# A mixture-of-experts layer: the 64 expert lists packed into 42 passes instead of 52, rows without a token skipped, and the last pass added from the matmul unit

## Chip, cores, metric

One core of one Trainium2 chip. The metric is the device time of one launch in microseconds (us), the median of several runs.

## What is computed

One decoder step for 512 prompt tokens, 16 meta tokens and 8 sample tokens of 1024 features: a state-space part and a retention part (not touched by the change), an output projection, and then a mixture of experts (MoE). Its core in the reference:

```python
scores = jax.nn.sigmoid((h @ w_router).astype(jnp.float32))
...
_, eidx = lax.top_k(jnp.where(emask, sel, -jnp.inf), TOP_K)      # 8 of 64 experts
...
hg = jnp.einsum('td,edf->tef', h, w_gate_e)                      # 1024 -> 256
hu = jnp.einsum('td,edf->tef', h, w_up_e)
act = jax.nn.silu(hg) * hu * gates[..., None]
routed = jnp.einsum('tef,efd->td', act, w_down_e)                # 256 -> 1024
shared = (jax.nn.silu(h @ w_gate_sh) * (h @ w_up_sh)) @ w_down_sh
```

The layer's output is x + routed + shared, and the final output is its rmsnorm. 520 tokens (the prompt and the samples) go through the experts, 8 experts each, so the lists of the 64 experts hold 4160 rows together. On the reference's own inputs the router gives, sorted by length, lists of 243, 175, 146, 130, 116, 105, 105, 105, 95, 89, ... rows; the 26th (counted from 0) has 64, the 59th 28 and the last 7. Everything is float32. The three matrices of one expert are 3 x 1024 KB, 201 MB for all 64.

## The kernel before

The first 400 us compute the two mixers, the output projection, the router and, on the chip, the ranking of the experts by the length of their lists. A **rank** below is the place of an expert in this order. The expert of a rank is read from a table (`order_i`) into a register, so the program is fixed and the experts are not.

The MoE stage works in **passes** (`UNITS`, `make_units`, L83). A pass has 128 row places. A list of rank 0 to 3 gets 256 places (two passes), one of rank 4 to 31 gets 128 places (a pass), and lists of rank 32 to 63 get 64 places each, two to a pass. That makes 52 passes (`NU`): 36 that hold one list and 16 that hold two. A *visit* (`VISITS`) is an expert in the order in which its weights are needed. What a list has beyond its places would be done afterwards in `overflow`, in a loop that is skipped when nothing is left.

What a pass u does, by engine:

- SyncE (SP) loads the weights (`sync_weights`, L358) into one of 6 slots of 3 MB. Visit v waits for the slot of visit v-6: gate and up for the last up matmul that used it (`pe_gu`), down for the last down matmul (`pe_down`).
- ScalarE (ACT) loads the pass's piece of the lists four passes ahead (`act_list`, L347), one DMA for each list of the pass, and copies one half of PSUM results.
- VectorE (DVE) makes from it the row indices and gates (`dve_meta`). A place without a token gets an index of 2048 (`DUMP`) or more. DVE also copies the other halves, and actT (L654).
- GpSimd (POOL) gathers the 128 rows of the tokens from `h2_rows` in HBM, three passes ahead (`pool_gather`, L440; `bounds_check` is 1543 there, so an index of 2048 and above is out of bounds), and scatters the 128 result rows into `sum_rows` in HBM with an addition (`pool_scatter`, L449; `bounds_check` is 2175 there, so the rows from 2048 on are written). Scatter u waits until scatter u-1 has landed.
- TensorE (PE) runs, in this order: the gate and up matmuls of u (`pe_up`), the transposes of the rows of u+1 (`pe_rows`), the down matmuls of u-1 (`pe_down`), the transposes of the activations of u (`pe_act`). All the matmuls are recorded at L912, row transposes at L929, activation transposes at L950. A matmul of float32 leaves two records in the trace.

A pair's two lists are in separate columns of the array (0 to 63 and 64 to 127) and in separate rows of a PSUM bank. Rows of its upper half go to a second copy of the sum, 1024 rows further (`ACC2`), because a token could stand in both lists, and two additions to one row in one DMA would lose one of them.

After the last pass POOL waits for the last scatter, asks for overflow, and sets `all_added`; then SP loads both copies of the sums (10 DMAs, L401), DVE adds them (L734), ACT squares them and takes the root (L534), DVE scales (L907), SP stores. The table of lists is filled with zeros in the first 60 us, as are the gaps between row 520 and row 1024 of `h2_rows` and `sum_rows`, through three more DMAs (L1202).

## Time and profile before

| | us |
|---|---|
| median of 3 runs (1156.03 to 1158.11) | 1157.16 |
| the profiled execution, its own time | 1158.64 |
| its span, from the first to the last instruction | 1156.8 |
| PE busy | 1013.1 (88%) |
| DVE, POOL, ACT busy | 435.0, 261.6, 200.5 |
| mean granted TensorE clock | 0.941 of full speed |

The profiled execution's time is 1.84 us more than its span. "Busy" is the union of an engine's instructions, and for DMA the mean over the core's 16 DMA engines. Of one more view: the DMA share of a stretch near or a little over 1 means that all 16 engines always had packets in work.

### The profile page before, as it was taken

How to read it: one execution, taken by the hardware profiler on the slowest of the kernel's cores; microseconds unless marked ns; L12 is line 12 of the kernel's file. 1: busy time of each engine (PE TensorE's matmuls, PEld its weight loads, DVE VectorE, ACT ScalarE, POOL GpSimd, SP SyncE). 2: the span in 40 equal slices, each digit the busy share in tenths (PEclk: the TensorE clock that was granted, in tenths of full speed). 3: DMA queues.
4: the chain of work that ended last, by engine and by line, in shares of the span. 5: the costliest groups of instructions: out<-in, count | busy, mean ns of one | idle time of the engine just before them, and what ended most of it. 6: DMA issues, size and time to landing. Idle time of an engine off the chain costs nothing.

```text
span 1156.8 us, 11769 instructions
## 1 busy us (share of the span) xinstructions
PE 1013.1 (88%) x3825; PEld 504.2 (44%) x3825; DVE 435.0 (38%) x1036; ACT 200.5 (17%) x401; POOL 261.6 (23%) x320
## 2 busy tenths in 40 slices
PE   5989987979888977899999979988999969997950
PEld 3564555556445533344444434433444424443420
DVE  6866467766936541223121212212122112221214
ACT  5150032312222211111111101111111101111112
POOL 2900056030300661021212112112021202222110
PEclk9989998989988988899999989999899979998995
DMA  9932020221353259699999999999999999999846
GB/s 330 407 148 74 1 73 1 91 67 74 109 206 126 74 227 415 258 356 367 380 368 380 367 386 383 366 381 380 373 375 349 377 379 353 340 371 369 293 87 225
DMA packets 72175, 308.98 MB, mean 267 GB/s; under 512 B 18529, under 2 KB 19585, under 8 KB 47153
## 3 DMA queue, kind: packets, MB, share of 16 engines
q1 hardware_dynamic: 48112, 261.07, 56.7%
q0 software_dynamic: 16256, 45.40, 16.2%
q10 hardware_dynamic: 7744, 1.73, 0.8%
q8 instruction: 32, 0.52, 0.2%
q14 instruction: 31, 0.25, 0.1%
HBM read 262.60 MB, written 55.79 MB: 275 GB/s over the span
## 4 chain that ended last, share of the span: by engine, by line
PE 68%; DMA 12%; DVE 8%; issue 6%; ACT 4%; POOL 2%; SPq 1%; POOLq 0%; DVEq 0%; ACTq 0%
PE bank L912 43%; PE bank L1839 20%; DMA sum_rows<-arena,xs 6%; PE bank L929 4%; DVE arena L1487 3%; DMA sum_rows<-arena 2%; POOL expert_lists L459 2%; DMA arena<-h_rows,xs 1%; PE bank L950 1%; DMA arena<-sum_rows 1%; ACT arena L1156 1%; ACT arena L1143 1%; DVE arena L1818 1%; DVE arena L1800 1%; DMA qkv_samples<-arena 1%
## 5 line engine op out<-in xcount | busy, mean ns | idle before, releaser
L912 PE MATMUL bank<-arena 128*128 128x512 f32 (+4 forms) x1890 | 630.2, 586 | 54.6 <-issue 34.2
L912 PEld LDWEIGHTS bank<-arena 128*128 128x128 f32 (+2 forms) x1890 | 249.2, 169 | 358.7 <-issue 343.6
L1839 PE MATMUL bank<-arena 128*128 128x512 f32 (+9 forms) x1208 | 308.3, 442 | 30.6 <-DVE arena L1487 8.3
L1839 PEld LDWEIGHTS bank<-arena 128*128 128x128 f32 (+4 forms) x1208 | 172.4, 191 | 160.0 <-issue 128.4
L449 POOL DMA_INDIRECT sum_rows<-arena,xs x52 | 81.7, 1571 | 497.8 <-DVE xs L667 301.0
L638 DVE SCALAR_TENSOR_TENSOR arena<-arena,xs,bank 128x256 f32<-128x256 f32 x52 | 34.7, 667 | 365.1 <-issue 326.6
L635 DVE COPY arena<-bank 128x512 f32<-128x512 f32 x52 | 36.0, 692 | 141.8 <-PE bank L912 130.8
L513 ACT ACTIVATE arena<-bank 128x256 f32<-128x256 f32 x52 | 20.0, 385 | 392.4 <-PE bank L912 287.3
L1487 DVE TENSOR_TENSOR arena<-arena 64x512 f32<-64x512 f32 (+8 forms) x79 | 69.6, 882 | 6.5 <-DMA arena<-o_samples 3.9
L440 POOL DMA_INDIRECT arena<-h_rows,xs x52 | 54.2, 1042 | 60.0 <-DVE xs L667 45.2
L929 PEld LDWEIGHTS bank<-ident,arena 128*128 128x128 f32 x416 | 47.3, 140 | 31.8 <-issue 28.0
L459 POOL DMA_INDIRECT expert_lists<-arena,ncim x40 | 40.0, 1000 | 91.5 <-issue 88.3
L507 ACT COPY arena<-bank 128x512 f32<-128x512 f32 x52 | 30.5, 586 | 152.4 <-PE bank L912 114.3
L929 PE MATMUL bank<-ident,arena 128*128 128x128 f32 x416 | 54.9, 275 | 0.2 <-DMA arena<-h_rows,xs 0.2
L626 DVE COPY arena<-bank 128x512 f32<-128x512 f32 x52 | 35.5, 682 | 13.6 <-DMA sum_rows<-arena 13.5
L499 ACT COPY arena<-bank 128x512 f32<-128x512 f32 x52 | 30.5, 586 | 34.6 <-PE bank L929 28.5
L950 PEld LDWEIGHTS bank<-ident,arena 128*128 128x128 f32 x104 | 13.3, 140 | 31.7 <-issue 31.2
L1295 POOL COPY prm<-prm 128x8 f32<-128x8 f32 x2 | 0.4, 188 | 118.1 <-PE bank L1839 97.2
L1487 DVE TENSOR_TENSOR arena<-bank,cosin 128x512 f32<-128x512 f32 (+1 forms) x24 | 14.4, 602 | 26.8 <-PE bank L1839 14.5
L654 DVE COPY arena<-bank 128x256 f32<-128x256 f32 x52 | 21.6, 415 | 0.0
L950 PE MATMUL bank<-ident,arena 128*128 128x128 f32 x104 | 20.7, 281 | 0.3 <-DVE arena L638 0.3
L1850 PE MATMUL bank<-ident,arena 128*128 128x128 f32 (+1 forms) x40 | 7.8, 383 | 13.3 <-DVE arena L1514 10.0
(230 smaller groups left out, 513.4 us busy)
## 6 DMA issues: line engine op xcount, KB each, us to landing
arena<-in_w_gate_e SPq DMA_DIRECT2D x64, 1024.0 KB, 20.4
arena<-in_w_up_e SPq DMA_DIRECT2D x64, 1024.0 KB, 33.6
arena<-in_w_down_e SPq DMA_DIRECT2D x64, 1024.0 KB, 30.8
arena<-in_w_in SPq DMA_DIRECT2D x5, 2048.0 KB, 12.4
expert_lists<-arena SPq DMA_DIRECT2D x1, 8482.5 KB, 28.8
sum_rows<-arena SPq DMA_DIRECT2D x9, 512.0 KB, 26.2
arena<-in_x_prompt SPq DMA_DIRECT2D x8, 512.0 KB, 5.7
arena<-in_w_out SPq DMA_DIRECT2D x2, 2048.0 KB, 8.2
```

Of the source, the lines that this page charges most:

```text
L440: pool.indirect_dma_start(xg[u % XBUF], None, h2_dram, bass.IndirectOffsetOnAxis(idx[:, u % IDX:u % IDX + 1].bitcast(U32), axis=0), bounds ...
L449: pool.indirect_dma_start(sum_dram, bass.IndirectOffsetOnAxis(idx[:, u % IDX:u % IDX + 1].bitcast(U32), axis=0), ys[u % 2], None, bounds_c ...
L459: pool.indirect_dma_start(tab, bass.IndirectOffsetOnAxis(dest[0:r_, n_, k:k + 1].bitcast(U32), axis=0), grow[0:r_, i, :], None, bounds_che ...
L499: nc.scalar.copy(xgT[u % 2][:, 0:4, :], bank[0][:, :].rearrange("p (k t) -> p k t", k=4)).then_inc(s("a_xgt"), 1)
L626: nc.vector.tensor_copy(xgT[u % 2][:, 4:8, :], bank[1][:, :].rearrange("p (k t) -> p k t", k=4)).then_inc(s("d_xgt"), 1)
L635: nc.vector.tensor_copy(ys[u % 2][:, 512:1024], bank[5][:, :]).then_inc(s("d_ys"), 1)
L638: return nc.vector.scalar_tensor_tensor(actg[b].rearrange("t (k p) -> t p k", k=2), sil[b].rearrange("t (p k) -> t p k", k=2), gate_col, g ...
L912: return nc.tensor.matmul(o, l, r, start=start, stop=stop, skip_group_check=True)
L929: t = nc.tensor.transpose(bank[k // 4][:, P * (k % 4):P * (k % 4) + P], xg[u % XBUF][:, P * k:P * k + P], ident[:])
L950: t = nc.tensor.transpose(bank[3][:, P * k:P * k + P], actg[u % 2][:, P * k:P * k + P], ident[:])
L1487: return v.tensor_tensor(o, a_, b_, op)
L1839: return nc.tensor.matmul(o, l, r, start=start, stop=stop, skip_group_check=True, **kw)
```

## The change

1. **Packing.** `CAPACITY` gives 256, 192, 160, 160 places to ranks 0 to 3, 128 to ranks 4 to 7, 96 to ranks 8 to 25, 64 to ranks 26 to 59 and 32 to ranks 60 to 63. Each pass is cut into blocks of one width (128, 64 or 32 columns): 9 passes of one whole block, 14 of two blocks of 64 (13 pairs of light lists, and the last 64 places of rank 1 beside a light list), 18 of four blocks of 32 (`thirds`: 96 places of one list in three blocks, and in the fourth 32 places of another, which in 12 of them is one half of a 64-place list spread over two passes), and the last pass with a light list alone in one block of 64. Together 42 passes.
2. **No spare rows.** A place without a token gets an index of 8192 (`FAR`) or more for gather and for scatter, and both DMAs now have `oob_is_err=False` and bounds that exclude it (519 and 1039). The second copy of `h2_rows` and the spare rows of `sum_rows` are gone, with their stores and the three DMAs of zeros; the two copies of the sum are 520 rows apart, and `ACCS` says which of them each list of a pass goes to.
3. **Tables.** The expert and the validity of each place of each pass come from 8 small matmuls more in `sort()` with a table of ranks that SP loads (`c_sel`), and fewer DVE operations in `sort_tables`. `dve_meta` has one small operation more.
4. **actT** is copied by ACT (`act_turn`), not DVE, between ACT's half of the down results and its list loads.
5. **The end.** The last pass (a light list alone) is not scattered. SP waits for the scatter of the last but one (`scattered` of 41) and loads both copies of the sums; POOL adds the two copies (L507 of the changed kernel); PE multiplies the result rows of the last pass with a one-hot matrix (`onehot`, 1 where the row of the pass belongs to the token), 8 matmuls of 128 x 512 and 4 of 8 x 256; DVE adds that from PSUM and goes on as before, tile by tile.

```diff
@@ make_units
-    for g in range(HEAVY // 2):
-        for r in heavy[2 * g:2 * g + 2]:
-            for first in range(0, rank_capacity(r), 128):
-                units.append(((r, 0, 128, first),))
-        units.append(((HEAVY + 2 * g, 0, 64, 0), (HEAVY + 2 * g + 1, 64, 64, 0)))
+CAPACITY = [256, 192, 160, 160] + 4 * [128] + 18 * [96] + 34 * [64] + 4 * [32]
+    thirds = lambda r: [(r, 32 * n, 32, 32 * n) for n in range(3)]
+    split = [[thirds(mids.pop(0)) + [(r, 96, 32, 32 * h)] for h in range(2)] for r in [light.pop(0) for _ in range(6)]]
+    both = [[thirds(mids.pop(0)) + [(r, 96, 32, 0)]] for r in least]
+    pairs = [[[(r, 64 * h, 64, 0) for h, r in enumerate(light[n:n + 2])]] for n in range(0, len(light), 2)]
@@ moe_sync
+            sp.wait_ge(s("pe_down"), NT + NU - 1)
+            sp.dma_start(gain_f, ins["final_norm"].partition_broadcast(P)).then_inc(s("ld_gain"), 16)
+            sp.wait_ge(s("scattered"), 16 * (NU - 1))
+            for n_, i in enumerate(LATE):
+                load_sums(sp, n_, f"ld_tok{i}")
             overflow(sp, sync_more)
-            sp.wait_ge(s("pe_down"), NT + NU)
-            sp.dma_start(gain_f, ins["final_norm"].partition_broadcast(P)).then_inc(s("ld_gain"), 16)
-            sp.wait_ge(s("all_added"), 1)
@@ pool_scatter
-            pool.indirect_dma_start(sum_dram, bass.IndirectOffsetOnAxis(idx[:, u % IDX:u % IDX + 1].bitcast(U32), axis=0),
-                                    ys[u % 2], None, bounds_check=DUMP + P - 1, compute_op=ALU.add
+            pool.indirect_dma_start(sum_dram, bass.IndirectOffsetOnAxis(idx_a[:, u % IDX:u % IDX + 1].bitcast(U32), axis=0),
+                                    ys[u % 2], None, bounds_check=NACC * TT - 1, oob_is_err=False, compute_op=ALU.add
                                     ).then_inc(s("scattered"), 16)
@@ moe_pool
-            for u in range(NU):
+            for u in range(NU - 1):
                 if u + XBUF < NU:
                     pool_gather(pool, u + XBUF)
                 pool_scatter(pool, u)
-            pool.wait_ge(s("scattered"), 16 * NU)
             overflow(pool, pool_more)
-            pool.memset(marks[:, 4:5], 0.0).then_inc(s("all_added"), 1)
+            for n_, i in enumerate(LATE):
+                r_ = rows_of(n_)
+                pool.wait_ge(s(f"ld_tok{i}"), 80 if i == TE else 64)
+                pool.tensor_tensor(fin[0][0:r_, n_, :], fin[0][0:r_, n_, :], fin[1][0:r_, n_, :], ALU.add
+                                   ).then_inc(s("pre_added"), 1)
@@ act_unit
+            act_turn(act, u)
             if u + LISTS < NU:
                 act_list(act, u + LISTS)
@@ moe_pe, after the last pass
+            for n_, i in enumerate(LATE):
+                if n_ == NT - 1:
+                    pe.wait_ge(s("d_sum"), 1)
+                rows = ys[(NU - 1) % 2]
...
+                    for hf in range(2):
+                        t = mmul(bank[LAST_BANK[n_] + hf][:, :], onehot[:, P * i:P * i + P], rows[:, 512 * hf:512 * hf + 512],
+                                 True, True)
+                t.then_inc(s("pe_last"), 1)
```

PE's order in the MoE stage, three passes of the kernel before (a list alone, a pair, a list alone). L912 is up (x8, or x16 for a pair) and down (x4, or x8), L929 the row transposes of the next pass, L950 the activation transposes:

```order
L912 MATMUL bank<-arena 128x512 x8
L929 MATMUL bank<-ident,arena 128x128 x8
L912 MATMUL bank<-arena 128x512 x4
L950 MATMUL bank<-ident,arena 128x128 x2
L912 MATMUL bank<-arena 64x512 x16
L929 MATMUL bank<-ident,arena 128x128 x8
L912 MATMUL bank<-arena 128x512 x4
L950 MATMUL bank<-ident,arena 128x128 x2
L912 MATMUL bank<-arena 128x512 x8
L929 MATMUL bank<-ident,arena 128x128 x8
L912 MATMUL bank<-arena 64x512 x8
L950 MATMUL bank<-ident,arena 128x128 x2
```

The same engine in the changed kernel, a pass of two blocks, one of four and one of two (L970 matmuls, L987 and L1008 the transposes; 32x512 is one block of 32 columns of the array):

```order
L970 MATMUL bank<-arena 64x512 x8
L1008 MATMUL bank<-ident,arena 128x128 x2
L970 MATMUL bank<-arena 32x512 x32
L987 MATMUL bank<-ident,arena 128x128 x8
L970 MATMUL bank<-arena 128x512 x4
L1008 MATMUL bank<-ident,arena 128x128 x2
L970 MATMUL bank<-arena 64x512 x16
L987 MATMUL bank<-ident,arena 128x128 x8
L970 MATMUL bank<-arena 32x512 x16
L1008 MATMUL bank<-ident,arena 128x128 x2
L970 MATMUL bank<-arena 32x512 x32
L987 MATMUL bank<-ident,arena 128x128 x8
```

The number of matmuls follows the number of blocks (32 up matmuls for four), and no transposes are added.

The end of the last passes on PE in the changed kernel, up to the question for overflow (TENSOR_LOAD):

```order
L970 MATMUL bank<-arena 32x512 x32
L987 MATMUL bank<-ident,arena 128x128 x8
L970 MATMUL bank<-arena 32x512 x16
L1008 MATMUL bank<-ident,arena 128x128 x2
L970 MATMUL bank<-arena 128x512 x8
L987 MATMUL bank<-ident,arena 128x128 x8
L970 MATMUL bank<-arena 32x512 x16
L1008 MATMUL bank<-ident,arena 128x128 x2
L970 MATMUL bank<-arena 64x512 x8
L970 MATMUL bank<-arena 128x512 x4
L1008 MATMUL bank<-ident,arena 128x128 x2
L970 MATMUL bank<-arena 64x512 x4
L437 TENSOR_LOAD xs
```

The passes 39 (up 32x512 x32), 40 (up 128x512 x8) and 41 (up 64x512 x8) need one new expert each, where of the last passes before the 52nd needs two.

The end of POOL's scatters, before:

```order
L449 DMA sum_rows<-arena,xs 2176x1024
L440 DMA arena<-h_rows,xs 128x1024
L449 DMA sum_rows<-arena,xs 2176x1024
L440 DMA arena<-h_rows,xs 128x1024
L449 DMA sum_rows<-arena,xs 2176x1024 x4
L412 TENSOR_LOAD xs
L412 ISA x2
L413 COMPARE_AND_BRANCH
```

and in the changed kernel, where the last three follow a last gather and the additions of the sums come behind the question for overflow (its loop of skipped passes is left out here):

```order
L470 DMA arena<-h_rows,xs 128x1024
L479 DMA sum_rows<-arena,xs 1040x1024
L470 DMA arena<-h_rows,xs 128x1024
L479 DMA sum_rows<-arena,xs 1040x1024 x3
L437 TENSOR_LOAD xs
L437 ISA x2
L438 COMPARE_AND_BRANCH
```

and further down:

```order
L441 REGISTER_ALU
L441 COMPARE_AND_BRANCH
L440 UNCONDITIONAL_BRANCH
L507 TENSOR_TENSOR arena<-arena 128x1024 x2
L507 TENSOR_TENSOR arena<-arena 8x1024
L507 TENSOR_TENSOR arena<-arena 128x1024 x2
```

The last pass has no scatter of its own, and POOL's five additions take its place.

## Rows read from the trace of the kernel before

**Rows 1.** the page: DMA share in 40 slices of 28.9 us (tenths)

```profile
DMA  9932020221353259699999999999999999999846
```

**Rows 2.** windows: us, busy PE, PEld, DVE, ACT, POOL, PEclk, DMA share, GB/s

```profile
466.40:1103.70 637.30, 602.37 (x2092) 269.42 (x2092) 136.54 (x389) 78.85 (x152) 129.17 (x99) 0.97 0.99 359
...
466.40:500.00 33.60, 33.08 (x107) 15.06 (x108) 9.15 (x30) 3.50 (x7) 3.65 (x3) 0.93 0.71 266
500.00:800.00 300.00, 290.07 (x1018) 129.72 (x1017) 66.52 (x197) 37.97 (x73) 65.42 (x50) 0.98 1.03 375
...
1124.80:1129.20 4.40, 0.00 (x0) 0.00 (x0) 0.00 (x0) 0.00 (x0) 0.00 (x0) 0.50 0.76 119
```

**Rows 3.** the page, DMA queues: packets, MB, share of 16 engines

```profile
q1 hardware_dynamic: 48112, 261.07, 56.7%
q0 software_dynamic: 16256, 45.40, 16.2%
```

**Rows 4.** the chain in order of time: start, length, what (x records)

```profile
583.17 6.87 PE bank L912 x16
590.04 0.87 PE bank L929 x8
590.91 3.44 PE bank L912 x8
...
594.57 6.87 PE bank L912 x16
...
559.78 7.02 PE bank L912 x32
```

**Rows 5.** PE groups by form, 416 to 460 us: xcount, busy, mean ns

```profile
L912 PE MATMUL bank<-arena 128*8 128x256 f32 x16 | 1.1, 380 | 0.3 <-DVE arena L852 0.3
```

**Rows 6.** SP's waits; the loads of in_w_down_e, issue to landing

```profile
SPq L344 <- PE bank L912: 284.3, 38, 15.0
...
DMA to landing us min/median/max: 4.9/30.8/39.8
```

**Rows 7.** the scatters (line 449), from issue to landing

```profile
DMA to landing us min/median/max: 6.1/10.4/12.1
```

**Rows 8.** timelines before the first pass, ACT and DVE

```profile
436.90 4.97 ACTq L354 DMA_DIRECT2D prm<-expert_lists  x5
...
388.55 1.28 DVE L734 TENSOR_TENSOR arena<-arena,bank 128x512 f32<-128x512 f32 x2
...
465.62 0.69 DVE L626 COPY arena<-bank 128x512 f32<-128x512 f32 x1 [13.47 <-DMA sum_rows<-arena]
```

**Rows 9.** timeline of the end: start, us, engine, line, operation [idle before]

```profile
1103.74 10.72 PE L912 MATMUL bank<-arena 128*64 128x512 f32 x40 [2.35 <-issue]
...
1114.49 0.69 DVE L635 COPY arena<-bank 128x512 f32<-128x512 f32 x1 [2.55 <-PE bank L912]
...
1123.16 1.54 POOL L449 DMA_INDIRECT sum_rows<-arena,xs  x1 [5.62 <-DMA sum_rows<-arena,xs]
...
1130.88 5.45 SPq L401 DMA_DIRECT2D arena<-sum_rows  x10
1136.63 1.23 DVE L734 TENSOR_TENSOR arena<-arena 128x1024 f32<-128x1024 f32 x1 [16.53 <-DMA arena<-sum_rows]
...
1140.26 2.35 DVE L734 TENSOR_TENSOR arena<-arena 128x1024 f32<-128x1024 f32 x2 [2.40 <-DMA arena<-sum_rows]
...
1145.60 1.23 DVE L734 TENSOR_TENSOR arena<-arena 128x1024 f32<-128x1024 f32 x1 [1.27 <-DMA arena<-sum_rows]
...
1146.86 1.06 ACT L534 ACTIVATE arena<-arena 128x1024 f32<-128x1024 f32 x1 [1.02 <-DVE arena L734]
...
1148.04 0.29 ACT L534 ACTIVATE stat<-stat 128x1 f32<-128x1 f32 x1
...
1152.48 1.28 DVE L907 SCALAR_TENSOR_TENSOR arena<-arena,stat 128x1024 f32<-128x1024 f32 x1
```

**Rows 10.** groups by form on POOL

```profile
L1329 POOL TENSOR_TENSOR arena<-arena 64x1024 f32<-64x1024 f32 x4 | 10.6, 2673 | 38.6 <-DVE arena L1800 38.6
```

More of the change, by code:

```diff
@@ L108, with make_accumulators @@
 IDX = 8
[L111 to L114 removed]
+def make_accumulators():
+    used = [-1] * NACC
+    chosen = []
+    for u, tiles in enumerate(UNITS):
+        ranks = list(dict.fromkeys(t[0] for t in tiles))
+        free = sorted(range(NACC), key=lambda a: used[a])[:len(ranks)]
+        for a in free:
+            used[a] = u
+        chosen.append(dict(zip(ranks, free)))
+    name = {a: n for n, a in enumerate(sorted(range(NACC), key=lambda a: -used[a]))}
+    return [{r: name[a] for r, a in c.items()} for c in chosen]
+ACCS = make_accumulators()
 def lists_landed(u):
@@ L2133, in shape_constants @@
     c["c_rt"] = rt
+    unit = np.zeros((P, P), np.float32)
+    sel = np.zeros((NE, NE + 4 * NU), np.float32)
+    sel[:, 0:NE] = e64
+    unit[:, 0:NU] = FAR
+    for u, tiles in enumerate(UNITS):
+        for r_, c0, width, first in tiles:
+            unit[c0:c0 + width, u] = first + np.arange(width)
+            unit[c0:c0 + width, 64 + u] = TT * ACCS[u][r_] - FAR
+            for q in range(c0 // 32, (c0 + width) // 32):
+                sel[:, NE + NU * q + u] = r_
+    c["c_unit"] = unit
+    c["c_sel"] = sel
     return c
```

270 lines of the change are left out of this document (152 added, 118 removed).

## The prediction

> **What bounds it now.** I read the DMA slices first, then windows of the MoE stage, the DMA queues, the chain, the waits and the end.
>
> The 16 DMA engines are full from the 18th slice to the 37th [rows 1]. From the first up matmul (466.4 us) to the last (1103.7) pass 637.3 us with a DMA share of 0.99; only the first 34 us leave air, at 0.71 [rows 2]. PE is close behind: a whole pass takes 11.40 us from up to up (583.17 to 594.57), a pair's up 7.02 instead of 6.87 [rows 4], so 52 passes are 595 us of work, and PE is busy in 602 of the 637 us. So two things nearly tie, and the reader should see that the transfers are the longer: SP waits 284 us for slots, but what it issues lands only a median 30.8 us later, where the quickest load takes 4.9 [rows 6]. Some 26 us of transfers are always ahead of a new load, so a freed slot does not make DMA idle, and DMA time is what the stage costs. Taking passes away from PE alone would give little.
>
> **Rows that are no longer moved (the main term).** The software queue moved 45.40 MB [rows 3]. 4160 list rows of 260 bytes are 1.08 MB, and the remaining 44.3 MB are 10,820 rows of 4096 bytes. The 52 scatters write 52 x 128 = 6656; that leaves 4160 for the gathers, exactly the rows with a token. So gathers skip the spare places already (their index is out of bounds) at no visible cost, and scatters write 6656 - 4160 = 2496 rows that are nobody's. The change skips these in the scatter too. What is such a row worth? The hardware queue's 261.07 MB took 56.7% of 1156.8 us, 656 us on all 16 engines, or 2.51 us per MB; a plain row then costs 0.165 us of one engine. The software queue took 16.2%, 2998 us of one engine; less 4160 gathered rows at 0.165 (686) and the lists at the same rate per byte (43), 2269 us remain for 6656 scattered rows, 0.341 each, about twice a plain one, which fits an addition that reads and writes. 2496 x 0.341 / 16 = **53.2 us** less. Ends: if a scattered row cost only the queue's mean (2998/10,816 = 0.277) it is 43 us; by the lone last scatter (4.4 us at a share of 0.76 [rows 2], 0.418 per row) 65 us. I take the middle, since the split is made from the whole run and the lone scatter runs with a latency that nothing covers.
>
> **Ten passes fewer (hidden).** The weights are the same 201 MB, the token rows the same 4160. On PE 42 x 11.4 = 479 us of work remain against 637 - 53 = 584 us of transfers, so the 114 us that PE saves turn into waits for weights. The cover is 105 us; if DMA were no longer the bound, this is what would show. Scatters wait for one another: one issue of 1.5 us and a median landing of 10.4 [rows 7, 9] make about 12 us a pass, 42 x 12 = 504, also below 584.
>
> **Blocks of 32 columns.** 18 passes run four blocks. I must know whether four blocks run side by side. The sample tile does it already: 16 records of 128x256 in four column groups take 1.1 us [rows 5]. A record of 512 columns takes 6.87/16 = 0.43 us, one of 256 would take 0.21; one after another the 16 would take 3.4 us, side by side 0.86 and the last one's run-out. So four blocks cost as one, and I charge 0 to 0.15 us a pass, under the cover. The Trainium skill speaks against this change: its page "TensorE: Matmul & The Clock Gate", section "Measured speedup vs the span model", gives 2.38 times for three column blocks, not 3. By that ratio each such pass would cost 1.26 times its 10.3 us of matmuls, 48 us in all, PE would come to 527 us, and the sum would stay as it is, with half the cover. The rows for 256 columns are better than that, and I go by them.
>
> **The end of the stage (given back).** The last three passes need one new expert each [the order above]. Three passes on PE are 34.2 us; three experts are 3 x 3.146 MB x 2.51 = 23.7 us of DMA, with 7 us for their rows 30.8. PE ends 3.4 us behind the transfers; and before, the last up matmul started when gate and up were there, 2.6 us (a third of an expert) before the transfers ended. **+6 us**; 0 to +10.
>
> **Before the first pass.** The first pass starts when the store of the shared result has landed (DVE's copy waited 13.5 us for it, to 465.6) [rows 8]; that store is issued before ACT's list loads and stands behind the same weights. ACT issues 11 list DMAs instead of 5 (4.97 us for 5, so +6 us), with its shared copies and SP's stores and the weights of visit 5 queued behind them; some 5 us of that is slack before 465.6. The tables have 8 small matmuls more and five DVE operations fewer, within 1 us. 2.6 MB of stores go away between 330 and 400 us and 6 MB of zeros in the first 60, where the chain runs through PE: 0. **+1 us**; -2 to +5. actT on ACT: 0.4 us behind a matmul block of 7 us, hidden.
>
> **The tail.** Before, from the copy after the last but one down (1114.49) to the end (1156.8) pass 42.3 us: its scatter, the last scatter, the question for overflow, 10 loads, additions, norms. Now, counted from the same copy: the scatter has landed by +8.7 (POOL's next instruction stood at 1123.16); loads take 5.7, 9.4 and 14.7 us to the first, second and last tile [rows 9], so +14.4, +18.1, +23.4. POOL adds five tiles at 2.67 us, the nearest row [rows 10]; its queue is the longer one: +17.1, +20.8, +23.5, +26.1, +28.8. DVE then adds the halves from PSUM, 1.3 us [rows 8], square and root 1.5, reciprocal 0.2, and from the last scaling to the end 4.3 us [rows 9]: +36.1. The 12 one-hot matmuls (two of 0.86 us a tile, twice that at the lower clock) fit between +6 and +23. Saved: **6.2 us**; 1 to 10. A rule of the Trainium skill bears on it: "SBUF — State Buffer", section "SBUF: two separate sides", says that GpSimd and a DVE operation with two SBUF inputs hold a shared port in turn, the other blocked. DVE's scaling (1.28 us, sum and gain) falls among POOL's additions three times: by the rule 3.8 us more, and a total of 1109. No row here has both at once in this form, so the sum is without it.
>
> **Sum.** 1158.6 - 53.2 + 6 + 1 - 6.2 = 1106.2 for a profiled execution; that one stood 1.5 us over the median of 1157.16, so **1105 us**.
>
> **Rivals.**
> (a) *DMA runs dry.* An expert spread over two passes holds its slot one pass (11.4 us) longer, for the 4 heaviest, the 6 split lists; pairs free two at once. Against it stand the 26 us of backlog; for it the first 34 us, where with few slots turning the share is 0.71 [rows 2]. At 1 to 3 us for each of the ten: +10 to +30, 1115 to 1135.
> (b) *Slower: four blocks run two by two* at 512 columns. Each of the 18 passes costs 10.3 us more, 185 in all, PE has 479 + 185 = 664 us and becomes the bound, 11 us over the 653 from first up to last down before; less the tail, 1163. It starts to decide at 5.8 us a pass (105/18), and makes the kernel slower from about 10. Rows 5 speak against it.
> (c) *The change does not do what it says:* a list exceeds its places and the overflow loop runs: the reference's list of rank 26 has just 64 rows for 64 places. One loop is two experts (16 us), gather, pass, scatter and new loads, 50 to 55 us without cover: about 1158, no change.
> (d) *More than the sum:* a scattered row is worth 0.418 and the end loses nothing: 1085 to 1092.
>
> **Chances.** Forecast (1092 to 1115) 0.67, (a) 0.16, (d) 0.09, (b) 0.04, (c) 0.04. Range: the ends of the main term, 43 and 65, give 1115 and 1093; most of (a) and the top of (d) added, 1090 to 1123. A measurement of this kernel tells 0.2% (2.3 us): faster 0.93, same 0.03, slower 0.04.
>
> **What would show it.** DMA share near 1 and no change of its rate from 500 us to the last load; the software queue at about 34 to 35 MB and 11.5 to 12% of the old span; PE busy in the stage down by over 100 us, with waits of up to 12 us before up matmuls of passes with two new experts; last up near 1055 to 1058; four-block up in 7.0 us; end of POOL's additions about 29 us behind the last but one down. Wrong: a DMA share well below 1 in the stage (a), up matmuls of 9 us or more (b), transposes and matmuls of an overflow pass after the 42nd (c).

## The result and the profile after

The changed kernel takes **1126.28 us** (median; 1125.68 to 1128.53), beside 1157.63 for the kernel before on the same chip: ratio 0.9722 [0.9698, 0.9746], 31 us faster. Forecast were 1105, with a range of 1090 to 1123. The direction was right, the size was not, and the time lies outside the range. The profiled execution took 1128.53 us, with a span of 1126.7.

The page of the changed kernel: DMA share and rate in 40 slices, and the DMA queues (packets, MB, share of 16 engines).

```profile
DMA  9720120231315119969999999999999999999735
GB/s 327 286 75 30 47 75 0 85 77 75 107 40 197 48 54 398 412 240 384 389 391 376 387 389 381 382 388 368 365 391 366 370 384 362 378 364 353 264 80 199
...
q1 hardware_dynamic: 46016, 252.34, 56.3%
q0 software_dynamic: 13232, 35.07, 11.9%
```

The software queue fell from 45.40 to 35.07 MB and from 16.2% to 11.9% [rows 3], as forecast. Yet the slices still read 9 up to the last load. Windows of the changed kernel: us, busy PE, PEld, DVE, ACT, POOL, PEclk, DMA share, GB/s; the first is the whole stage from first to last up matmul.

```profile
471.20:1076.20 605.00, 517.54 (x3024) 194.32 (x3024) 103.67 (x323) 73.95 (x162) 102.05 (x78) 0.93 0.96 363
...
471.20:505.00 33.80, 33.37 (x163) 13.31 (x164) 8.78 (x30) 4.14 (x9) 3.65 (x3) 0.94 0.74 273
505.00:1039.00 534.00, 447.21 (x2608) 167.50 (x2606) 88.08 (x274) 64.96 (x142) 93.54 (x72) 0.92 1.00 377
1039.00:1076.20 37.20, 36.97 (x254) 13.51 (x254) 6.82 (x19) 4.84 (x11) 4.87 (x4) 0.96 0.68 231
```

The stage shrank from 637.3 us [rows 2] to 605.0: 32.3 us, where the prediction had 53.2 - 6 = 47.2. PE is busy 85 us less and waits for weights instead. SP's queue waits more for places than before, and what it issues lands a median 25.7 us later instead of 30.8 [rows 6]. The changed kernel's waits (us in total, times, longest) and landing of in_w_down_e:

```profile
SPq L367 <- PE bank L970: 387.6, 34, 18.2
SPq L363 <- PE bank L970: 21.6, 5, 8.7
...
DMA to landing us min/median/max: 4.9/25.7/38.2
```

Four column blocks run side by side, as forecast. In the changed kernel's timeline, late in the stage: a four-block up, its down, and the up of the next pass with its one wide block (start, us, line, columns, records).

```profile
1052.57 7.07 PE L970 MATMUL bank<-arena 128*32 128x512 f32 x64
1060.60 3.64 PE L970 MATMUL bank<-arena 128*32 128x512 f32 x32
1064.45 7.03 PE L970 MATMUL bank<-arena 128*128 128x512 f32 x16
```

The end, the changed kernel's timeline (start, us, engine, line, operation [idle before]):

```profile
1088.48 1.54 POOL L479 DMA_INDIRECT sum_rows<-arena,xs  x1 [9.38 <-DVE arena L680]
...
1094.91 4.54 SPq L433 DMA_DIRECT2D arena<-sum_rows  x10
1099.99 2.34 POOL L507 TENSOR_TENSOR arena<-arena 128x1024 f32<-128x1024 f32 x1 [9.97 <-DMA arena<-sum_rows]
...
1103.02 9.25 POOL L507 TENSOR_TENSOR arena<-arena 128x1024 f32<-128x1024 f32 x4 [0.69 <-DMA arena<-sum_rows]
...
1106.79 6.56 DVE L959 SCALAR_TENSOR_TENSOR arena<-arena,stat 128x1024 f32<-128x1024 f32 x1
...
1113.27 1.69 DVE L782 TENSOR_TENSOR arena<-arena,bank 8x256 f32<-8x256 f32 x4
...
1115.07 1.28 DVE L959 SCALAR_TENSOR_TENSOR arena<-arena,stat 128x1024 f32<-128x1024 f32 x1
```

From the copy after the last but one down (1086.97) to the end pass 39.7 us, 42.3 before; forecast were 36.1. The 6.56 us of DVE is a scaling that takes 1.28 elsewhere; it ends 1.1 us after POOL's last addition (1112.3).

**The account.** Forecast 1106.2 for a profiled execution. The stage gave 14.9 us less than forecast, the tail 3.6 less, and the first up matmul came at 471.2 instead of 467.4, 3.7 late: 1106.2 + 14.9 + 3.6 + 3.7 = 1128.4.

The stage's 14.9 us split further at the last landing of gate and up weights (from the trace's landing records). Before, they landed at 1103.6, 0.1 us ahead of the last up; after, at 1067.3, 8.9 us ahead of it, and PE had no waits left from 1039 us on (36.97 us busy of 37.20, above). So, counted from the first up, the weights were in 41.1 us sooner (637.2 to 596.1) where 53.2 were forecast, and the end gave back 8.8 us where 6 were. The open question was the first of these.

### The profile page after: what moved, and what is told of

Read it like the earlier page. It is cut to its first block, busy times and chain, and to the rows that moved or that the text cites. A ratio compares the mean times of both kernels' runs of the same rounds, so it can differ in the third digit from the quotient of the medians.

```text
span 1126.7 us, 13692 instructions
## 1 busy us (share of the span) xinstructions
PE 937.6 (83%) x4773; PEld 432.3 (38%) x4773; DVE 406.4 (36%) x974; ACT 196.5 (17%) x413; POOL 246.3 (22%) x303
## 3 DMA queue, kind: packets, MB, share of 16 engines
q0 software_dynamic: 13232, 35.07, 11.9%
## 4 chain that ended last, share of the span: by engine, by line
PE 69%; issue 11%; DVE 8%; DMA 6%; ACT 4%; POOL 2%; SPq 1%; POOLq 0%; DVEq 0%; ACTq 0%
PE bank L970 43%; PE bank L1915 20%; PE bank L987 4%; DVE arena L1563 3%; DMA sum_rows<-arena 2%; POOL expert_lists L489 2%; PE bank L1008 1%; ACT arena L1236 1%; ACT arena L1223 1%; DVE arena L782 1%; DMA arena<-in_x_prompt 1%; DMA qkv_samples<-arena 1%; DVE arena L1894 1%; DVE arena L1876 1%; DMA arena<-sum_rows 1%
## 5 line engine op out<-in xcount | busy, mean ns | idle before, releaser
L970 PE MATMUL bank<-arena 128*32 128x512 f32 (+6 forms) x2930 | 554.3, 615 | 116.6 <-issue 87.0
L970 PEld LDWEIGHTS bank<-arena 128*32 128x32 f32 (+3 forms) x2930 | 190.4, 135 | 417.5 <-issue 396.0
L479 POOL DMA_INDIRECT sum_rows<-arena,xs x41 | 64.6, 1575 | 489.6 <-DVE bb L705 426.5
L683 DVE SCALAR_TENSOR_TENSOR arena<-arena,xs,bank 128x256 f32<-128x256 f32 x42 | 28.2, 672 | 387.6 <-issue 351.1
L555 ACT ACTIVATE arena<-bank 128x256 f32<-128x256 f32 x42 | 16.2, 385 | 393.6 <-PE bank L970 393.6
L680 DVE COPY arena<-bank 128x512 f32<-128x512 f32 x42 | 29.1, 692 | 119.3 <-PE bank L970 119.3
L470 POOL DMA_INDIRECT arena<-h_rows,xs x42 | 43.6, 1039 | 56.7 <-DVE bb L705 45.0
L987 PEld LDWEIGHTS bank<-ident,arena 128*128 128x128 f32 x336 | 36.7, 140 | 31.0 <-issue 30.9
L549 ACT COPY arena<-bank 128x512 f32<-128x512 f32 x42 | 24.6, 586 | 126.2 <-PE bank L970 111.3
L987 PE MATMUL bank<-ident,arena 128*128 128x128 f32 x336 | 45.3, 278 | 0.0
L671 DVE COPY arena<-bank 128x512 f32<-128x512 f32 x42 | 29.0, 690 | 9.7 <-DMA sum_rows<-arena 9.7
L535 ACT COPY arena<-bank 128x512 f32<-128x512 f32 x42 | 24.6, 587 | 29.5 <-PE bank L987 25.1
L782 DVE TENSOR_TENSOR arena<-arena,bank 128x512 f32<-128x512 f32 (+3 forms) x30 | 16.7, 580 | 26.2 <-POOL arena L507 11.8
L1563 DVE TENSOR_TENSOR arena<-bank,cosin 128x512 f32<-128x512 f32 (+1 forms) x24 | 14.4, 601 | 27.8 <-PE bank L1915 14.5
L1008 PEld LDWEIGHTS bank<-ident,arena 128*128 128x128 f32 x84 | 9.2, 140 | 31.6 <-issue 31.2
L1405 POOL TENSOR_TENSOR arena<-arena 64x1024 f32<-64x1024 f32 x4 | 10.6, 2674 | 38.5 <-DVE arena L1876 38.5
## 6 DMA issues: line engine op xcount, KB each, us to landing
arena<-in_w_down_e SPq DMA_DIRECT2D x64, 1024.0 KB, 25.7
```

Of the source, the lines that this page charges most:

```text
L470: pool.indirect_dma_start(xg[u % XBUF], None, h2_dram, bass.IndirectOffsetOnAxis(idx[:, u % IDX:u % IDX + 1].bitcast(U32), axis=0), bounds ...
L479: pool.indirect_dma_start(sum_dram, bass.IndirectOffsetOnAxis(idx_a[:, u % IDX:u % IDX + 1].bitcast(U32), axis=0), ys[u % 2], None, bounds ...
L535: nc.scalar.copy(xgT[u % 2][:, 0:4, :], bank[0][:, :].rearrange("p (k t) -> p k t", k=4)).then_inc(s("a_xgt"), 1)
L671: nc.vector.tensor_copy(xgT[u % 2][:, 4:8, :], bank[1][:, :].rearrange("p (k t) -> p k t", k=4)).then_inc(s("d_xgt"), 1)
L680: nc.vector.tensor_copy(ys[u % 2][:, 512:1024], bank[5][:, :]).then_inc(s("d_ys"), 1)
L683: return nc.vector.scalar_tensor_tensor(actg[b].rearrange("t (k p) -> t p k", k=2), sil[b].rearrange("t (p k) -> t p k", k=2), gate_col, g ...
```

## Experiments

Eighteen kernels were run, in six groups. Times are medians; the kernel before, run beside them, took 1159.2 to 1160.2 us.

### Rows, by number (e1, e2)

e1 writes the rows of the empty places again, and changes nothing else but for one store more of 0.5 MB, which fills the spare rows:

```
-    v.tensor_scalar(else_a, else_a, float(FAR), None, ALU.add)
+    v.tensor_scalar(else_a, else_a, rconst[:, 4:5], None, ALU.add)      # NACC * TT + t
-    bounds_check=NACC * TT - 1, ...
+    bounds_check=NACC * TT + P - 1, ...
```

> The changed kernel, but the scatters write their rows without a token again, to 128 spare rows behind the sums (41 scatters, 1116 such rows), as the kernel before did. If DMA time is what the stage costs, 1116 x 0.341 / 16 = 24 us come back, less a few us that fill the places where DMA now runs dry: 1126 + 15 to 24 = 1141 to 1150. Rival, that the 42 passes made the gain and the rows are hidden: 1126 to 1130.

e2 is the kernel before with the empty rows left out: `bounds_check=DUMP - 1, oob_is_err=False` in its scatter.

> The kernel before with 52 passes, but its scatters skip the rows without a token (a bound of 2047 and no error). DMA loses 2496 rows, 53 us. The theory that DMA bounds and PE is close behind: PE has 595 to 602 us of work in the 637 us between first and last up matmul, so no more than 35 us can be won, and the skipping alone gives most of what the whole change gives: 1122 to 1135. Rival, that the passes matter: 1145 to 1157.

Measured: e1 **1127.17** (1125.43 to 1128.05), e2 **1152.89** (1151.17 to 1155.6; ratio 0.9948 [0.9929, 0.9967]). The queue's bytes moved as they should. Of e1, and then of e2:

```profile
q0 software_dynamic: 13232, 39.63, 13.9%
```

```profile
q0 software_dynamic: 16256, 35.20, 11.9%
```

So e1 moves 4.56 MB more in 2.0% more of 16 engines' span (23 us by the mean), and takes the same time. e2 takes 4.3% away (50 us), and gains 6 (4 to 8). The main term of the prediction fell: an empty row costs the engines its full time and the kernel next to nothing.

### Order of the loads, and the end (e3, e4, e5, e6, e7)

e3 keeps every load, but SP issues gate/up and down loads in the order in which PE frees their places; before, a gate/up load whose place is free stands behind a down load that still waits.

```
+    parts = [(LAST_UNIT[v_ - NSLOT] + 1.5 * down, v_, down) for v_ in range(NSLOT, NE) for down in (0, 1)]
+    for _, v_, down in sorted(parts):
+        sync_part(sp, v_, down)          # waits for pe_down or pe_gu, then issues its one part
-    for v_ in range(5, NE):
-        sync_weights(sp, v_)
```

> The changed kernel with SP's weight loads in the order in which PE frees their places: the gate and up loads of both experts of a two-expert pass before the down load of the first, which waits for a down matmul one pass later. Theory: the 10 us of dry DMA in the middle of the stage (shares of 0.7 to 0.9 in stretches of 5 us around 680, 795, 853 and 875 us) come from a free gate/up place behind a waiting down load; with the new order they go: 1113 to 1120. Rival, that all six slots are in use there and the order changes nothing: 1124 to 1128.

e4 moves the additions of the two copies of the sums from POOL to DVE (the loop at L507 is left out, `tt(fin[0].., fin[0].., fin[1].., ALU.add)` stands ahead of DVE's own additions).

> The changed kernel with the two copies of the sums added by DVE (1.23 us a tile in the kernel before) and not by POOL. Theory: DVE's scaling of the first tile, 6.56 us where 1.28 is usual, stood behind POOL's additions; without them the tail falls by 4 to 7 us: 1119 to 1122. Rival, that DVE becomes the longer queue (five times 1.23 more on it): 1125 to 1129.

e5 is e2 with e3's order, e6 is e3 with e4's additions, e7 is e3 with e1's rows.

> The kernel before (52 passes) with the empty rows left out of its scatters and with its weight loads issued in the order in which PE frees the places. Theory (the kernel before is bound mainly by PE; with half the weights left out it only fell to 1113.6, so all its waits for weights are worth 46 us): the order saves at most what it saved after the change, 1140-1150. Rival (transfers set the stage before, and order and rows together open it): 1125 or less.

> The changed kernel with the loads in the order in which PE frees the places (-11.5 alone) and the five additions of the end on DVE instead of POOL (-2.6 alone). The two lie in different stretches, so they should add: 1110-1113. Rival (the copies land later with the earlier end of the stage, or the order's gain takes the same slack): 1114-1116.

> The changed kernel with the weight loads issued in the order in which PE frees their places (1114.8 measured) and with the scatters writing the rows of the empty places to spare rows again, as before the change (about 24 us of the DMA engines' time more). Theory (rows cost nothing as long as the engines have dry places; with the loads in order they have few, mid-stage share 1.02): some of the 24 us now show, 1120-1135. Rival (rows never cost, what counts is when places come free): 1113-1117.

Measured: e3 **1114.83** (ratio 0.9609 [0.9578, 0.9641]), e4 **1123.72** (0.9685 [0.9659, 0.9712]), e5 **1148.66**, e6 **1112.80** (1110.27 to 1115.5), e7 **1114.42**. The order is worth 11.5 us after the change and 4.2 before it (e2 to e5), so it held back the changed kernel more than the kernel before. SP's waits in e3, where 387.6 + 21.6 us became 107:

```profile
SPq L363 <- PE bank L981: 77.5, 18, 9.3
...
SPq L367 <- PE bank L981: 29.5, 9, 9.8
```

e7 says that the empty rows stay free even where the loads are asked for early: my expectation for it fell as well, since it still took the mean over the engines. In e4 DVE's scaling takes its usual time, beside its own additions of the copies (1.23 us, POOL 2.3):

```profile
1103.49 1.28 DVE L777 TENSOR_TENSOR arena<-arena,bank 128x512 f32<-128x512 f32 x2
1104.69 0.15 DVE L955 RECIPROCAL stat<-stat 128x1 f32<-128x1 f32 x1
1104.88 1.28 DVE L956 SCALAR_TENSOR_TENSOR arena<-arena,stat 128x1024 f32<-128x1024 f32 x1
1106.08 1.21 DVE L777 TENSOR_TENSOR arena<-arena 8x1024 f32<-8x1024 f32 x1
```

### What binds: weights, matmuls, token rows (e8, e9, e11, e12)

e8 and e9 load half of each weight row from the seventh expert on, in the kernel after and before (`wexp[slot][:, 2048 * kind:2048 * kind + 1024]`, and likewise for down). e12 is e3 with `for k in range(0, KD, 2)` in the up products. e11 is e3 with `bounds_check=0` in the scatter.

> The changed kernel, but from the seventh expert on only the first half of each weight row is loaded (half of gate, up and down; the products of those experts are wrong). Everything else, the waits included, stays. Theory (after the change the stage waits for weights, and PE alone would need 42 passes of 11.4 us = 479 us from first to last up where 605 are measured): 1126.5 falls by 90 to 125, to 1000-1035. Rival (something else than the weights sets a pass, such as scatters that wait for one another at about 12 us, or the clock): falls by under 60, over 1065.

> The kernel before with the same half of the weights left out. Theory now held (the kernel before was bound mainly by PE's 52 passes, 595 us of 637, and only some 40 us of its stage were waits for weights): 1157.5 falls by 30 to 50, to 1107-1128. Rival, the prediction's own reading (transfers set the stage): PE would still hold it at 595, so the fall is the same 40; but then the half of the bytes should do no more than leaving out the spare rows by that reading (53 predicted, 6 measured). What tells is the pair: the difference before minus after becomes 10 passes of PE, 105 to 120 us, where it is 31 with all the weights.

> The changed kernel with the loads in release order (1114.8), and its scatters write none of the 4160 token rows but those of token 0 (the experts' share of all other tokens is left out of the sums). By the prediction's price that takes 88 us of the DMA engines' time away. Theory (time of rows on the DMA engines lies beside the weight stream and costs nothing; what counts is when weights are asked for and land): 1105-1115, of which up to 5 by shorter landings and a shorter last scatter. Rival (DMA time does count once the loads are in order): 1030-1080.

> The changed kernel with the loads in release order (1114.8), and the up and gate products run over every second group of 128 features only (half of those matmuls left out, about 3.4 us of 11.4 us a pass, 144 us of PE in all). Asks what the weight stream alone would take. Theory (the stage is now set by the stream of weights, 64 experts at about 384 GB/s with the rows): PE's saving mostly turns into waits, 1080-1105. Rival (PE and the places it frees are coupled one to one): 1000-1050.

Measured: e8 **1005.89**, e9 **1113.58**, e11 **1030.92** (1028.97 to 1031.79), e12 **1106.20**. With half the weights PE never waits: from 500 to 900 us it is busy for 400 us of 400 in both. So PE's passes alone would need 1006 us after and 1114 before; of the 108 us between them 105 lie between first and last up (486.4 and 591.2 us), and are the ten passes. The rows are all still moved in e8 and e9, so it is through the weights that they cost time. e12 leaves half of the up matmuls out (PE's busy time falls by 112 us, from 933 to 821, less than the 144 at the full clock, since its granted clock fell from 0.92 to 0.83) and gains 8.6: the transfers hold the changed kernel. And e11 refutes what e1, e2 and e7 had made me believe: some 4120 token rows fewer (16.9 MB, from 35.07 to 18.20) save **84 us**, where the price of the prediction, shared over 16 engines, gives 88. Empty rows are free, and token rows are not. What was left to look at was in which partitions they lie.

### Rows, by place (e13, e14)

A list fills its block of places from below. Worked out from the lengths of this input's lists (243, 175, 146, 130, 116, ... 16, 7, in all 4160) and the places of each pass, the rows with a token in the 16 groups of 8 partitions are, from group 0 to group 15:

| | gathered (the token rows) | scattered, fullest group |
|---|---|---|
| before, 52 passes | 410 408 394 386 371 333 283 241 315 254 215 188 166 110 54 32 | 416 (every place) |
| e2, e5 | the same | 410 |
| after, 42 passes | 336 336 336 332 318 282 231 216 300 246 210 192 308 241 169 107 | 328 |
| e1, e7 | the same | 328 (every place) |

If each DMA engine moves the rows of one such group, the fullest engine has as many rows with the empty ones as without: the empty places lie on engines that have time. (The last pass is not scattered after the change, hence 328 and not 336.) e13 and e14 are e3 with some token rows not scattered:

```
e13: +  for g in (6, 7, 9, 10, 11, 13, 14, 15): unit[8 * g:8 * g + 8, 64:64 + NU] += FAR
e14: +  unit[1::2, 64:64 + NU] += FAR
```

> The changed kernel with the loads in release order (1114.8); its scatters leave out the token rows that lie in eight of the sixteen groups of 8 partitions (partitions 48-63, 72-95, 104-127), 1612 of the 4160 rows. New theory (each of the 16 DMA engines moves the rows of one group of 8 partitions, the lists fill their places from below, so the groups at the start of a block carry most rows, 336 scattered in the fullest against 106 in the emptiest, and the weights wait for the fullest engine): these are light groups, so nothing changes, 1112-1117. Rival 1 (rows go round the engines in turn, place by place): the fullest engine falls from 292 to some 180 rows, 1075-1090. Rival 2 (the mean over the engines counts; 4160 rows were worth 84 us): 1612 rows are worth 33, 1078-1086.

> The same kernel, but its scatters leave out the token rows in the odd partitions, 2063 of the 4160 rows. New theory (groups of 8 partitions): every engine loses half of its scattered rows, the fullest 168, worth half of what all rows were worth: 1065-1080. Rival 1 (partition by partition in turn): the engines of the even partitions keep all their rows, 1110-1117. Rival 2 (the mean counts): 2063/4160 of 84 us, 1070-1076.

Measured: e13 **1120.09** (1116.51 to 1121.03), e14 **1067.45** (1065.66 to 1068.45). Windows from 500 to 900 us and the software queue of e3, e13 and e14, in this order:

```profile
500.00:900.00 400.00, 340.71 (x2014) 124.64 (x2016) 67.48 (x213) 49.07 (x107) 70.68 (x54) 0.92 1.02 384
```

```profile
500.00:900.00 400.00, 338.62 (x2031) 125.48 (x2030) 67.94 (x214) 49.46 (x108) 70.74 (x54) 0.93 0.99 370
...
q0 software_dynamic: 13232, 28.48, 9.2%
```

```profile
500.00:900.00 400.00, 364.13 (x2218) 135.96 (x2210) 75.01 (x234) 54.86 (x120) 75.87 (x58) 0.96 1.02 401
...
q0 software_dynamic: 13232, 26.69, 8.8%
```

Nearly the same number of rows is gone from both (6.6 and 8.4 MB). Taken from the light groups they save nothing (e13 is even 5 us slower, which I can't explain); taken evenly, with 164 of 328 gone from the fullest group, they save 47 us, 0.29 us each (the 168 and 2063 of the expectation count the last pass too, which is not scattered; without it they are 164 and 2049). Both rivals, by partition in turn and the mean over the engines, wanted 25 us or more from e13.

The landing records of the trace show the engines apart. Each load reports 16 times, once for each part. From the first to the last part of a down load pass, in the median of the loads behind 500 us:

| kernel | us from first to last part |
|---|---|
| before; e5 (order, no empty rows); e17 (the same, spread, below) | 21.2; 26.9; 14.7 |
| after; e3 (order); e6 (order, DVE additions) | 14.9; 24.2; 24.1 |
| e13 (light groups left out); e16 (spread and turned, below) | 25.4; 13.2 |
| e8 and e9 (half the weights) | 3.1 and 2.1 |

PE waits for the last. The gap tells that the engines are unevenly loaded, and is no price: e3 has a wider one than the changed kernel and is 11.5 us faster, since its loads are asked for earlier.

**The groups are not 8 neighbours.** In e13 eight of the 16 groups of neighbours keep no scattered row, so eight parts should come early. Ten do: in 53 of 57 loads the widest gap lies behind the tenth part, which lands 2.1 us after the first, the eleventh 19.2 us. A grouping that fits puts four neighbours together with the four that lie 32 partitions further (0 to 3 with 32 to 35, and so on; 64 to 67 with 96 to 99). Then six groups of e13 keep 290 to 326 scattered rows, four keep 164 and six none: ten light ones. Counted so, the fullest group has 395 gathered rows before and 330 after (scattered 416 and 326), close to the 410 and 336 of the table, so the argument stands on either. e2 fits it too: its fullest group scatters 395 rows instead of 416, which at 0.29 us are 6 us, as measured, where 8 neighbours give six rows and 2 us. Other groupings with the same ten and six are not excluded. What e13 and e14 do show is that the partitions don't go round the engines in turn, and that the mean over the engines is not what counts.

### Moving rows, leaving nothing out (e15, e16, e17, e18)

e15 is e6 with each list read into its places spread out, and the table of valid places changed to match:

```
-    tab_list[bass.ds(e, 1), first:first + width, :].rearrange("a c w -> (a c) w")
+    tab_list[bass.ds(e, 1), first:first + width, :].rearrange("a (x y) w -> (a y) x w", x=4)
...
-    unit[c0:c0 + width, u] = first + np.arange(width)
+    unit[c0:c0 + width, u] = first + c_ % 4 * (width // 4) + c_ // 4
```

e16 also turns the blocks: the n-th pass of four blocks has them at (c0 + 32 n) mod 128. e18 chooses the turn of each pass so that the groups of 8 fill evenly; for this the lengths of this input's lists are written into the kernel (`LENGTHS`), and other inputs would get other numbers. e17 is e5, the kernel before, with the lists spread as in e15.

> Loads in release order and DVE additions (1112.8), and each list is read into its places spread out: place c of a block of w gets row (c mod 4) * w/4 + c div 4, so that the rows of a short list lie over all the groups of its block; nothing left out. Theory (fullest engine counts): the fullest group has 311 rows instead of 336 (the groups within a block even out, the blocks don't), 25 rows at 0.4 to 0.5 us gathered and scattered: 1099-1104. Rival (place does not matter): 1111-1114; lists that cost more to load in pieces: up to 1116.

> As the one before, and in the passes of four blocks the blocks are turned by 32 columns from one such pass to the next, so that the part-filled block lies on other engines each time; nothing left out. The fullest group now has 285 rows instead of 336: 51 rows at 0.4 to 0.5 us make 20 to 25 us: 1088-1095 by the theory of the fullest engine, 1111-1116 by the rival that place does not matter.

> The kernel before (52 passes) with empty rows left out of the scatters and loads in release order (1148.7 together), and now its lists read into their places spread out, as in e15. By groups of 8 partitions the fullest engine falls from 410 rows to 308, fewer than the 336 of the changed kernel; PE keeps all 52 passes. If the fullest engine was what held the kernel before, 102 rows at 0.25 to 0.45 us are 25 to 45 us, down to the 1114 of the half weights at the lowest: 1114-1124, and the change's gain would be had without a pass less. If PE's 52 passes held it, 1140-1149.

> As e16 (1100.3), but the turn of each pass of four or two blocks is chosen by the lists' lengths so that the groups of 8 partitions fill evenly: fullest 275 rows instead of 285. At 0.25 us a row (from e16: 51 rows, 12.5 us) to 0.45: 1096-1099. Rival (the fullest engine no longer counts, passes and their waits do): 1099-1102.

The fullest group by gathered rows, in groups of 8 neighbours and of 4 and 4; the stage is first to last up in the profiled execution:

| kernel | 8 | 4 and 4 | first up at; stage, us | us (range) |
|---|---|---|---|---|
| e5, before, order, no empty rows | 410 | 395 | 467.7; 627.5 | 1148.66 (1147.86 to 1149.85) |
| e17, the same, spread | 308 | 291 | 469.1; 591.1 | **1110.35** (1109.78 to 1110.69), 0.9564 [0.9543, 0.9586] |
| e6, after, order, DVE additions | 336 | 330 | 468.2; 595.0 | 1112.80 (1110.27 to 1115.5) |
| e15, the same, spread | 311 | 304 | 472.3; 586.9 | 1110.69 (1107.99 to 1112.23) |
| e16, and turned | 285 | 281 | 476.4; 574.6 | 1100.27 (1097.09 to 1103.73) |
| e18, and evened | 275 | 277 | 472.6; 574.2 | **1095.53** (1094.97 to 1100.16), 0.9447 [0.9423, 0.947] |

**e17 decides.** The kernel before keeps its 52 passes and is now 16 us faster than the changed kernel with its 42, and level with e15, which has 42 passes and the same order and spreading. Windows from 500 to 900 us of e5, and of e17:

```profile
500.00:900.00 400.00, 379.70 (x1339) 170.39 (x1339) 86.87 (x253) 50.32 (x97) 86.38 (x66) 0.98 1.00 365
```

```profile
500.00:900.00 400.00, 400.00 (x1425) 179.31 (x1424) 92.70 (x269) 54.09 (x104) 89.50 (x69) 1.00 1.03 388
```

PE goes from 380 busy us to 400 of 400, at the full clock, and the same transfers run at 388 GB/s instead of 365; the time is that of e9, so PE's passes now hold it. My bound for e17, 1114, was missed by 4 us to the good side.

e15 gave 2 us where 9 to 14 were expected (its range overlaps that of e6), and e16 12.5 where 18 to 25 were. The stage gave nearly what was promised, 8.1 us for 25 rows and 20.4 for 51. The rest was given back ahead of the stage. A list that is read spread out is dearer to issue. The list loads of e6, and of e16 (duration min/median/max in ns, first and last start):

```profile
L377 ACTq DMA_DIRECT2D prm<-expert_lists x110: 322/323/592, 438.5 to 1028.4; - x110
```

```profile
L383 ACTq DMA_DIRECT2D prm<-expert_lists x110: 547/1162/1257, 441.5 to 1016.2; - x110
```

ACT issues 11 of them ahead of its share of the first copies. The first pass begins 4 us later in e15 and e18 than in e6, and 8 us later in e16; the lists are the same in all three, so the other 4 us of e16 are not theirs (its granted clock from 150 to 190 us was 0.83, as in the changed kernel, and 0.91 in e6, e15 and e18; see e10). Reading only the later lists spread might win back the first 4; it wasn't tried.

e18 is the best version, 62 us under the kernel before and 31 under the changed one. Its time lies just under the expected range, but that was luck: its stage is that of e16 (574.2 and 574.6 us), and the 5 us between the two came from the earlier start. The ten rows by which the groups of 8 were to fall saved nothing; in groups of 4 and 4 they are four rows.

### The start (e10)

e10 is the changed kernel with three stores of zeros of 2 MB each put back at the start (to rows that nobody reads), as the kernel before has them.

> The changed kernel with the three stores of 2 MB of zeros at the start put back (to rows that nobody reads), with their waits. Asks where the 4 us went by which the first expert pass starts later after the change (466.4 to 471.2). Theory (the start is then busier and the clock that TensorE is granted shifts its phases, as in the kernel before): first up back at 467 to 468, 1122-1125. Rival (the 4 us are of the tables or the lists): no change or slower, 1126-1130.

Measured: **1125.37** (1122.54 to 1126.28), too near to 1126.28 to be told from it. Its first up started at 467.0, as hoped, but e7, without the stores, started at 465.8. Among the kernels that share this part the start moves between 465.8 and 471.2. Most of the late ones were granted less clock between 150 and 190 us (e8 was not). That stretch in the changed kernel, and in e10, as windows:

```profile
150.00:190.00 40.00, 33.21 (x160) 23.42 (x160) 22.84 (x35) 10.08 (x21) 28.20 (x69) 0.83 0.05 18
```

```profile
150.00:190.00 40.00, 32.38 (x171) 22.36 (x170) 25.35 (x38) 11.98 (x24) 29.99 (x71) 0.91 0.04 15
```

The stores are not shown to be the cause, and what moves these phases of the clock stays open.

## Why the prediction was wrong

**The main term (-53.2) is the step that failed**, in its last division: "2496 x 0.341 / 16". The price of 0.341 us for a scattered row was a little high (e14 has 0.29, e11 0.26 or more). Sharing it out over 16 engines was wrong, because a load has landed only when its slowest engine is through, and nearly all of the 2496 empty rows lay on engines that were waited for by nobody: taking them away is worth 6 us before (e2) and 1 or nothing after (e1, e7), not 53. What the change really did is to move the token rows: 42 passes whose blocks of 32 fill more evenly have 336 gathered and 328 scattered in the fullest group instead of 410 and 416. By the prediction's own prices that is 88 x 0.341 + 74 x 0.165 = 42.2 us (41.4 in groups of 4 and 4), and the weights were in 41.1 us sooner. With this term the sum would have been 1117 for the profiled execution. By the prices of e14 and e15 to e17 (0.29 scattered, 0.3 to 0.4 for both, so about 0.1 gathered) it is 88 x 0.29 + 74 x 0.1 = 33. That the first comes out so near is in part luck, since the order of the loads, worth 11.5 us after the change and 4.2 before it, stands in no term.

How much of the gain the passes have is argued and not shown: no run has 42 passes with the rows of the old packing. Against a large share stand e17 (38 us with no pass less) and e12.

**"A freed slot does not make DMA idle, and DMA time is what the stage costs"** was half right. The transfers did hold the stage (e12, e8), but the 26 us of backlog were those of the fullest engines; the others were through up to 15 or 21 us earlier (after, before), as the parts of one load show (that they then stood idle is not seen directly). And an earlier request does help: -11.5 in e3. A DMA share of 0.99 [rows 2] hid both. I had read a share near 1 as all 16 engines always at work; e13 has 0.99 while ten parts of each load land 17 us and more ahead of the other six. It is a mean of the time that packets take, and it was 1.02 in e3, 1.03 in e7 and 0.99 in e13 for times within 6 us of each other.

**Ten passes fewer (hidden)**: right. e17 reaches 1110 with all 52 passes, and e12 gains 8.6 us from half of the up matmuls. The passes matter only below that: the kernel before could not have gone under 1110 to 1114 (e9, e17), the one after has 1006 (e8).

**Blocks of 32 columns**: right. Four blocks take 7.07 us at the full clock, 7.03 for one full-width up. The Trainium skill, "TensorE: Matmul & The Clock Gate", section "Measured speedup vs the span model", gives 2.38 times for three; nothing of that loss is seen in these rows.

**The end of the stage (+6)**: right in kind and a little small. The last up started 8.9 us behind the last landing of gate and up weights, where before it was 0.1: +8.8.

**Before the first pass (+1)**: measured +4.7 (466.4 to 471.2), inside the bound of -2 to +5. It is not from the lists that were feared: the first copies waited for the store of the shared result as before, and the delay came up far ahead of them: the same matmuls run 1.3 us later at 77 us, 2.9 at 156 and 4.6 at 250, and 4.5 at 384 (see e10).

**The tail (-6.2)**: measured -2.6, inside the bound of 1 to 10. The mechanism that the prediction left out of its sum did occur. In the trace DVE's scaling took 6.56 us beside POOL's additions instead of 1.28, and without them 1.28 again (e4, -2.6 us). The Trainium skill, "SBUF — State Buffer", section "SBUF: two separate sides", has GpSimd and a DVE operation with two SBUF inputs shut each other out; the trace agrees, the scaling ending 1.1 us after POOL's last addition. The prediction's estimate by that rule was 39.9 us for this stretch, and 39.7 were measured, but that is luck. POOL's additions were through 25.3 us after the copy, where 28.8 were forecast (2.3 us a tile and not 2.67, and earlier loads). From there to the end it took 14.4 us instead of 7.3: DVE was held once for 5.3 us, not three times for 1.28, and then had four of the five scalings and three of the sums still to do.

**Rivals.** (a), DMA running dry, had the range 1115 to 1135 and the right time, by a mechanism that is at most partly this one: some engines were through early, but for their rows and not for the slots of lists spread over two passes (the order of the loads, e3, is the nearest to it). (b), (c) and (d) did not occur. The range was too narrow since both its ends for the main term kept the division by 16: they varied the price of a row, never who pays it.

## What to carry to other kernels

Where rows are gathered or scattered by index, ask in which partitions they lie and not only how many they are: here the fullest group held up every load that shares the engines, and rows in light groups were free. Find the groups by leaving out chosen partitions and counting the early parts, as in e13. A mean DMA share near 1 says neither that less traffic will help nor that fewer passes won't; a wide gap between the landings of the parts of one load is a sign of uneven engines. In a queue that waits in order, issue loads in the order in which their places come free.

## What the runs showed of the hardware

- Parts of one load of 1 MB, issued together, landed 14.9 us (after), 21.2 us (before) and 25.4 us (e13) apart in the median, and 3.1 us where half the weights were left out (e8).
- With the scattered rows of partitions 48 to 63, 72 to 95 and 104 to 127 left out (e13), ten of the 16 parts landed within 2.1 us and the other six from 19.2 us on.
- A scattered row of 4096 bytes in the fullest group costs 0.26 to 0.29 us of the kernel's time (e11: at least 84 us for 328; e14: 47 for 164), gathered and scattered 0.3 to 0.4 (e15, e16, by the stage; e17 at least 0.375).
- TensorE was granted 1.00 (2.4 GHz) from 500 to 900 us wherever it never waited (e8, e9, e17), and on the mean 0.91 to 0.98 where it had gaps, 0.83 in e12. In the changed kernel an up took 8.4 to 9.9 us after 16 of 19 waits, and 7.1 after the other three.
- A DVE scaling of 128 x 1024 took 6.56 us beside POOL's additions and 1.28 us without them (e4).
- The issue of a small load took ACT 0.32 us with rows in sequence and 1.16 us with its rows spread in four strides (e6, e16; medians).
